# Mixing stage: two rotation tables scaled later, first swaps in PSUM, index pairs and value transposes later, top-k rounds spread

## Chip, cores and metric

One NeuronCore of one Trainium2 chip. The metric is the device time of one execution, in microseconds. TensorE is PE, VectorE is DVE, ScalarE is ACT and GpSimd is POOL in the rows.

## What is computed

Two blocks in a row on 512 tokens of width 1024. The first has a gated MLP, banded attention and two squared-ReLU MLPs. The second has two SwiGLU MLPs, a gated projection, and between the MLPs the mixing stage that this change is about. Cut to what matters:

```python
z = rms_norm_2(h, mix_norm) @ w_in
(aq, ak, av, iq, ik, iw, rq, rk, rv, rg, ga, gb) = jnp.split(z, split_points, axis=-1)
aq, ak, iq, ik = rope(aq), rope(ak), rope(iq) * 64 ** -0.5, rope(ik)      # 8, 1, 8, 1 heads of 64
rel = relu(einsum('bqhd,bsd->bqhs', iq, ik)); score = einsum('bqhs,bqh->bqs', rel, iw * 8 ** -0.5)
sel = top_k(where(admissible, score, -1e30), 128)                         # n_sel = min(256, 512 // 4)
y_a = softmax(aq @ ak[sel] / 8) @ av[sel]
rq, rk = rope(rq), rope(rk)                                               # 4 heads of 128
y_r = group_norm_heads(retention(rq, rk, rv)) * silu(rg)
merged = sigmoid(ga) * (y_a @ w_branch_a) + sigmoid(gb) * (y_r @ w_branch_b)
h = h + merged @ w_out
```

`rope` multiplies each head by a cosine and adds its swapped halves times a sine. The top 128 of up to 512 scores of a query are found in 16 rounds of 8.

## The kernel before

Activations lie feature-major: 128 features by 512 tokens a tile. Weights come as units of 128 x 1024 in fp32, are split into a high and a low part, and each product is three matmul passes (high x high, low x high, high x low; lines 435 to 437) over 8 tiles of contraction: 24 matmuls of 512 columns into one PSUM bank (`product`, `three_passes`). Most units are split by ScalarE (high) and VectorE (low). Units 256 to 294, those of the mixing stage up to the gates, are split by POOL: `high = raw * 1` (line 378) and `low = raw - high` (line 381), as soon as PE has finished the unit that held the slot before. SyncE's queue loads the raw units.

The engines run programs of their own that meet in semaphores; no scheduler stands between them, so the order of work on each engine is the order in the code. Four banks (0 to 3) take the units in turn: unit u waits until unit u - 4 is evacuated (semaphore `evacuated`).

On PE the mixing stage runs like this. First the units of the index queries (heads 0 to 3), of the index key (4) and of value and index weight (5, "avw"). Then units 6 to 10 (attention queries and key), with index work between their 40 tiles (`beside_heads`): one transposition of the value/weight unit (`transpose_avw`, line 760, bank 7) and 16 index pairs (`index_pair`, line 774, banks 4 to 7; four pairs for each of four query tiles t, with 128, 256, 384 and 512 keys). Then come eight retention units `ret_qk`, the retention values as two halves of four units each (`half_by_banks`, line 505, banks 0 to 3, bank by bank), and the gate stage: for each of four heads two gate units, retention scores, values (line 827) and transposes of the normalized result (line 838). The sparse attention stage follows.

VectorE evacuates each rotated unit in three instructions: `cosine_part` (line 1647, the unit's bank times the cosine table into T), then, after ScalarE's `swap_halves` (line 1170: copies of 32 or 64 rows from the unit's bank to `swapped(n)`), `sine_part`: the swapped half times the sine table (line 1652, frees the unit's bank) and the sum (line 1654). `swapped(n)` is a tile of T in SBUF for n below 10 and PSUM bank 4 or 5 for the retention units. The four tables `ROT` are first multiplied by the norm's reciprocal, which lies spread in PSUM bank 5 (line 1639). Line 1662 evacuates the value/weight unit. Index pairs pass through ScalarE's ReLU (line 1183, four buffers) and VectorE's `index_adds` (lines 1677, 1680), which sum 8 heads for each t into SC and then fill the inadmissible corner (line 1684). ScalarE copies SC to MK. `take(first, rounds)` is the top-k: a round is one maximum of 8 (line 1704) and one replacement (line 1705); rounds 0 to 15 work on 256 keys, 16 to 31 on 384, 32 to 47 on 512. `token_major(half, VT)` evacuates a value half in four instructions (line 1572). In the gate stage `mask(t)` turns SC and MK into an additive mask (lines 1723, 1725, 1726) ahead of `ret_norm(h)` (line 1761 writes YN).

Of the kernel before, what the change touches and what calls it, by code (L numbers as in the profile page):

```python
# [23 lines left out]
ALU = mybir.AluOpType  # L24
# [7 lines left out]
TT = SEQ // P  # L32
# [3 lines left out]
HD = 64  # L36
# [62 lines left out]
PAIRS = 4  # L99
# [58 lines left out]
def program(nc, xT, weights, gains, cols, lng, lnb, bs, wsT, rel, pos, ident_d, decay, pT, out):  # L158
    with ExitStack() as ctx:
        def at(name, kb, shape, dt=F32):  # L160
            return nc.alloc_sbuf_tensor_at(name, shape, dt, offset=16512 + int(kb * 1024))
# [15 lines left out]
        AQIQ = at("AQIQ", 64, [P, 8, SEQ])  # L177
        AK = at("AK", 80, [P, SEQ])
# [43 lines left out]
        ROT = at("ROT", 188, [P, 4, SEQ])  # L222
# [11 lines left out]
        COS64, SIN64, COS128, SIN128 = (ROT[:, n, :] for n in range(4))  # L234

        PS = ctx.enter_context(nc.psum_tensor("PS", [P, 8, SEQ], F32))

        def sem(name):
            return ctx.enter_context(nc.semaphore(name))
# [28 lines left out]
        dve_self, act_self = sem("dve_self"), sem("act_self")  # L268
# [32 lines left out]

        def swapped(n):

            return T[:, n % 2 * 2 + 1, :] if n < 10 else PS[:, 4 + n % 2, :]

        def ret_bank(c):
# [3 lines left out]
        def n_of(t):  # L310

            return P * (t + 1)
# [93 lines left out]
        def _(pe):  # L406
# [304 lines left out]
            for s in range(steps + 1):  # L711
                j = 2 * DT + 2 + 4 * s
# [50 lines left out]
            def index_pair(m):  # L763

                t, a = divmod(m, PAIRS)
                if m == 0:
                    pe.wait_ge(rotated, 5)
                if m == 1:
                    pe.wait_ge(index_ready, 1)
                if m >= 2:  # L770
                    pe.wait_ge(relu_done, 2 * m - 2)
                for hh in range(2):
                    r = slice(hh * HD, hh * HD + HD)
                    nc.tensor.matmul(PS[:, 4 + m % 2 * 2 + hh, 0:n_of(t)], AQIQ[r, 4 + a, t * P:t * P + P],
                                     IK[r, 0:n_of(t)], start=True, stop=True).then_inc(index_done, 1)

            def beside_heads(j):

                if j == 1:
                    transpose_avw()  # L780
                if j % 2 == 1 and j // 2 < TT * PAIRS:
                    index_pair(j // 2)
            for s in range(5):
                product(DT, XH, XL, after=lambda k: beside_heads(s * DT + k))
            for s in range(8):
# [112 lines left out]
            for s in range(first_step, last_step + 1):  # L898
                j = 4 * (s - first_step)
# [50 lines left out]
        def _(act):  # L950
# [3 lines left out]
            ta, me = Count(to_act), Count(act_self)  # L954
# [174 lines left out]
            for s in range(DT * TT):  # L1129
                p, t = divmod(s, TT)  # L1130
# [45 lines left out]
            def relus(first, last):  # L1176

                for n in range(first, last):
                    t = n // 8
                    act.wait_ge(index_done, n + 1)  # L1180
                    if n >= 4:
                        act.wait_ge(index_added, n - 3)
                    S.activation(RELU[:, n % 4, 0:n_of(t)], PS[:, 4 + n % 4, 0:n_of(t)], ACT.Relu)\
                     .then_inc(relu_done, 1)
            relus(0, 10)
            for t in range(TT):
                swap_halves(5 + t, heads + 6 + t, 32)
                act.wait_ge(scores_masked, t + 1)
                if t:
                    c = slice(off(t), off(t) + n_of(t))  # L1190
                    S.activation(MK[:, c], SC[:, c], ACT.Copy).then_inc(work_copied, 1)
                relus(8 * t + 10, min(8 * t + 18, 32))
            swap_halves(9, heads + 10, 32)
            for n in range(8):
                swap_halves(10 + n, FIRST["ret_qk"] + n, 64)
# [38 lines left out]
            for s in range(first_step, last_step):  # L1234
                p, t = divmod(s - first_step, TT)
# [63 lines left out]
        def _(dve):  # L1299
            dve.sem_inc(evacuated, SLOTS)  # L1300
            V = nc.vector
            done = Count(units_done, SLOTS)
            me, ao, ss = Count(dve_self), Count(act_out), Count(ss_ready)
# [294 lines left out]
            for s in range(DT * TT):  # L1598
                p, t = divmod(s, TT)
                n = n_of(t)  # L1600
# [34 lines left out]
            recip()  # L1635
            sp_.next()
            dve.wait_ge(ri_copied, rc.next())
            for n in range(4):
                V.tensor_tensor(ROT[:, n, :], ROT[:, n, :], PS[:, 5, :], ALU.mult).then_inc(dve_self, 1)
            dve.wait_ge(dve_self, me.next(4))  # L1640

            def cosine_part(n, cos, scale):


                if n >= 2:
                    dve.wait_ge(rotated, n - 1)
                V.scalar_tensor_tensor(T[:, n % 2 * 2, :], unit(), scale, cos, ALU.mult, ALU.mult).then_inc(turned, 1)

            def sine_part(n, dst, sin, scale):

                dve.wait_ge(act_out, ao.next())
                V.scalar_tensor_tensor(swapped(n), swapped(n), scale, sin, ALU.mult, ALU.mult).then_inc(evacuated, 1)
                dve.wait_ge(evacuated, FIRST["mix_heads"] + n + 1 + (n > 4) + SLOTS)
                V.tensor_tensor(dst, swapped(n), T[:, n % 2 * 2, :], ALU.add).then_inc(rotated, 1)

            cosine_part(0, COS64, HD ** -0.5)
            for n in range(4):
                cosine_part(n + 1, COS64, HD ** -0.5 if n < 3 else 1.0)
                sine_part(n, AQIQ[:, 4 + n, :], SIN64, HD ** -0.5)
            sine_part(4, IK[:], SIN64, 1.0)  # L1660
            dve.wait_ge(rotated, 4)
            V.tensor_tensor(T[:, 2, :], unit(), RI[:], ALU.mult).then_inc(evacuated, 1)
# [6 lines left out]
            def index_adds(t, first, last):  # L1669

                s = SC[:, off(t):off(t) + n_of(t)]
                for h in range(first, last):
                    n = 8 * t + h
                    w = AVW[:, t, HD + h:HD + h + 1]
                    dve.wait_ge(relu_done, n + 1)
                    if h == 0:
                        V.tensor_scalar(s, RELU[:, n % 4, 0:n_of(t)], w, None, ALU.mult).then_inc(index_added, 1)
                    else:
                        dve.wait_ge(index_added, n)
                        V.scalar_tensor_tensor(s, RELU[:, n % 4, 0:n_of(t)], w, s, ALU.mult, ALU.add)\  # L1680
                         .then_inc(index_added, 1)
                if last == 8:
                    dve.wait_ge(index_added, 8 * t + 8)
                    V.memset(s[0:CH, n_of(t) - CH:n_of(t)], NEG).then_inc(scores_masked, 1)
            index_adds(0, 0, 8)
            for t in range(TT):
                cosine_part(5 + t, COS64, HD ** -0.5)
                if t < TT - 1:
                    index_adds(t + 1, 0, 2)
                sine_part(5 + t, AQIQ[:, t, :], SIN64, HD ** -0.5)  # L1690
                if t < TT - 1:
                    index_adds(t + 1, 2, 8)
            cosine_part(9, COS64, 1.0)
            sine_part(9, AK[:], SIN64, 1.0)

            def take(first, rounds):


                for r in range(first, first + rounds):
                    t = 1 + r // 16  # L1700
                    if r % 16 == 0:
                        dve.wait_ge(work_copied, t)
                    work = MK[:, off(t):off(t) + n_of(t)]
                    link(V.max(TOP[:], work))  # L1704
                    link(V.match_replace(work, TOP[:], work, TAKEN))  # L1705

            for n in range(8):
                scale = 1.0 if n % 2 == 0 else P ** -0.5
                cosine_part(10 + n, COS128, scale)
                take(3 * n, 2)  # L1710
                sine_part(10 + n, R1[:, n, :], SIN128, scale)
                take(3 * n + 2, 1)
            take(24, 15)
            token_major(0, VT)
            take(39, 9)
            token_major(1, VT)

            def mask(t):


                c = slice(off(t), off(t) + n_of(t))
                ok = SC[:, c]
                link(V.tensor_scalar(ok, ok, 0.5 * NEG, None, ALU.is_gt))
                if t:
                    link(V.scalar_tensor_tensor(ok, MK[:, c], 0.5 * TAKEN, ok, ALU.is_lt, ALU.mult))
                V.tensor_scalar(MK[:, c], ok, -NEG, NEG, ALU.mult, ALU.add).then_inc(dve_self, 1)
                me.next()
# [12 lines left out]
            def two_bank_unit(u, dst):  # L1740

                dve.wait_ge(units_done, done.next())
                assert done.n == u + 1 + SLOTS
                V.tensor_tensor(dst, PS[:, 2 + u % 2, :], RI[:], ALU.mult).then_inc(evacuated, 1)
# [35 lines left out]
            ret_decay(0)  # L1780
            for h in range(4):
                two_bank_unit(rg0 + 2 * h, GT[:, 2 * h % 4, :])
                mask(h)
                ret_norm(h)
                two_bank_unit(rg0 + 2 * h + 1, GT[:, (2 * h + 1) % 4, :])
                if h < 3:
                    ret_decay(h + 1)
                ret_gated(h)
# [9 lines left out]
            for s in range(first_step, last_step):  # L1798
                p, t = divmod(s - first_step, TT)
                n = n_of(t)  # L1800
# [209 lines left out]
```

## Time and profile before

| | |
|---|---|
| runs | 2521.54 us median of 3 (2517.85 to 2522.76) |
| profiled execution | 2520.23 us, span 2518.4 us |
| mean granted clock of TensorE | 0.976 |
| busy share of the span | PE 95%, VectorE 54%, ScalarE 31%, POOL 18% |
| chain that ended last | PE 83%, VectorE 11%, ScalarE 3%, issue 2% |

The rotated units, values and gates of the mixing stage lie at about 1602 to 1854 us of the span. Times in the rows are from the span's start. The busy time of PE is modelled at the end of each matmul, so start-to-start distances say more than its busy share. A row of a timeline ends with the idle time of the engine before it and with what ended that.

### The profile page before, as it was taken

Reading aid. Unit: us, or ns where it says so; the run is one execution under the profiler, and the core shown is the slowest. Engines: PE = TensorE matmul, PEld = TensorE weight load, DVE = VectorE, ACT = ScalarE, POOL = GpSimd, SP = SyncE. Lnnn points to the kernel's source line nnn. Section 1 sums busy time; section 2 is a strip of 40 time slices with the busy share of each in tenths; the row PEclk is TensorE's granted clock in tenths of the full one; section 3 lists DMA queues with packets and bytes.
Section 4 is the critical chain, followed back from the end, with each engine's and each line's share of the span. In section 5 each row is a group of like instructions: output and inputs, shape, how many; then the busy total and the mean of one; then the engine's idle time right before and its main releaser. Section 6 shows DMA issues by size and latency. Waiting matters only on the chain.

```text
span 2518.4 us, 28995 instructions
## 1 busy us (share of the span) xinstructions
PE 2399.2 (95%) x10924; PEld 1934.3 (77%) x10924; DVE 1370.1 (54%) x1951; ACT 783.0 (31%) x1242; POOL 446.5 (18%) x203
## 2 busy tenths in 40 slices
PE   6789999997999899999999999998999999999997
PEld 5677888876766788888788888766877888888886
DVE  5666444446467644434555435789664454444465
ACT  2114323222233333223332223341244343222233
POOL 6670000003545200000000000456540000000000
PEclk8899999997999999999999999999999999999999
DMA  4232433321222233333143332223211343333221
GB/s 169 68 91 67 117 99 94 96 71 50 83 81 84 67 105 96 93 98 102 53 118 100 99 89 81 74 67 93 67 55 55 100 127 91 109 94 99 86 78 54
DMA packets 64833, 221.94 MB, mean 88 GB/s; under 512 B 7504, under 2 KB 9680, under 8 KB 64592
## 3 DMA queue, kind: packets, MB, share of 16 engines
q1 hardware_dynamic: 59184, 208.17, 27.9%
q10 hardware_dynamic: 5536, 12.19, 1.5%
q8 instruction: 80, 1.31, 0.2%
q14 instruction: 33, 0.27, 0.0%
HBM read 218.23 MB, written 2.10 MB: 87 GB/s over the span
## 4 chain that ended last, share of the span: by engine, by line
PE 83%; DVE 11%; ACT 3%; issue 2%; DMA 0%; POOL 0%; ACTq 0%; DVEq 0%; POOLq 0%
PE PS L435 23%; PE PS L437 22%; PE PS L436 22%; PE PS L454 3%; PE PS L531 2%; PE PS L458 1%; DVE SS L1344 1%; DVE MK L1705 1%; PE PS L681 1%; DVE SC L1680 1%; PE PS L505 1%; PE PS L702 1%; PE PS L691 1%; DVE TOP L1704 1%; PE PS L827 1%
## 5 line engine op out<-in xcount | busy, mean ns | idle before, releaser
L435 PE MATMUL PS<-XH,WH 128*128 128x512 f32 x1632 | 647.2, 397 | 19.6 <-DVE T L1542 12.5
L437 PE MATMUL PS<-XH,WL 128*128 128x512 f32 x1632 | 637.0, 390 | 0.0
L436 PE MATMUL PS<-XL,WH 128*128 128x512 f32 x1632 | 636.6, 390 | 0.0
L1332 DVE TENSOR_TENSOR WL<-RAW,WH 128x1024 fp32r<-128x1024 f32 (+3 forms) x308 | 362.2, 1176 | 224.3 <-ACT WH L977 219.7
L378 POOL TENSOR_TENSOR WH<-RAW,ONES 128x1024 fp32r<-128x1024 f32 x91 | 182.7, 2008 | 1437.3 <-DVE WL L1332 735.9
L977 ACT ACTIVATE WH<-RAW 128x1024 fp32r<-128x1024 f32 (+3 forms) x312 | 315.2, 1011 | 354.6 <-DVE M L1449 202.4
L435 PEld LDWEIGHTS PS<-XH,WH 128*128 128x128 f32 x1632 | 307.2, 188 | 101.3 <-issue 22.8
L435 PE MATMUL PS<-HH,WH 128*128 128x512 f32 x928 | 364.1, 392 | 2.6 <-DVE HL L1418 2.6
L437 PE MATMUL PS<-HH,WL 128*128 128x512 f32 x928 | 361.4, 389 | 0.0
L436 PE MATMUL PS<-HL,WH 128*128 128x512 f32 x928 | 361.2, 389 | 0.0
L437 PEld LDWEIGHTS PS<-XH,WL 128*128 128x128 f32 x1632 | 307.1, 188 | 65.1
L436 PEld LDWEIGHTS PS<-XL,WH 128*128 128x128 f32 x1632 | 307.5, 188 | 60.8
L381 POOL TENSOR_TENSOR WL<-RAW,WH 128x1024 fp32r<-128x1024 f32 x91 | 226.6, 2490 | 7.1
L435 PEld LDWEIGHTS PS<-HH,WH 128*128 128x128 f32 x928 | 174.2, 188 | 47.6 <-issue 9.1
L437 PEld LDWEIGHTS PS<-HH,WL 128*128 128x128 f32 x928 | 174.2, 188 | 36.5
L436 PEld LDWEIGHTS PS<-HL,WH 128*128 128x128 f32 x928 | 174.3, 188 | 35.2
L1418 DVE TENSOR_TENSOR HL<-T,HH 128x512 fp32r<-128x512 f32 x108 | 74.8, 692 | 127.4 <-ACT HH L1040 92.7
L1344 DVE TENSOR_TENSOR SS<-SS,T 128x512 f32<-128x512 f32 x91 | 85.0, 934 | 24.6 <-ACT T L983 24.6
L1037 ACT ACTIVATE T<-T 128x512 f32<-128x512 f32 x64 | 40.5, 632 | 185.0 <-DVE T L1425 185.0
L1449 DVE TENSOR_TENSOR M<-PS,M 128x512 f32<-128x512 f32 x48 | 33.1, 691 | 107.2 <-PE PS L437 106.8
L1052 ACT ACTIVATE HH<-T 128x512 fp32r<-128x512 f32 x44 | 27.8, 632 | 184.8 <-DVE T L1440 184.8
L1425 DVE SCALAR_TENSOR_TENSOR T<-PS,RI 128x512 f32<-128x512 f32 x64 | 44.2, 690 | 69.6 <-PE PS L437 61.6
(237 smaller groups left out, 2732.8 us busy)
## 6 DMA issues: line engine op xcount, KB each, us to landing
RAW<-in_weights SPq DMA_DIRECT2D x379, 512.0 KB, 3.5
RAW<-in_weights SPq DMA_DIRECT2D x16, 384.0 KB, 3.1
H<-in_xT ACTq DMA_DIRECT2D x8, 256.0 KB, 8.4
BIAS<-in_rel ACTq DMA_DIRECT2D x8, 256.0 KB, 3.5
RAW<-in_weights SPq DMA_DIRECT2D x8, 256.0 KB, 2.6
out<-R ACTq DMA_DIRECT2D x8, 256.0 KB, 2.2
BIAS<-in_rel ACTq DMA_DIRECT2D x8, 224.0 KB, 3.9
DECAY<-in_decay ACTq DMA_DIRECT2D x1, 1024.0 KB, 4.9
```

What stands on the lines that cost most here:

```text
L378: nc.gpsimd.tensor_tensor(high[:, 0:w], raw, ONES[:, 0:1].to_broadcast([P, w]), ALU.mult).then_inc(high_split, 1)
L381: nc.gpsimd.tensor_tensor(low[:, 0:w], raw, high[:, 0:w].bitcast(F32), ALU.subtract).then_inc(weights_split, 1)
L435: nc.tensor.matmul(PS[:, bank_, :], high[:, w], xh[:, k, :], start=(k == 0), stop=False)
L436: nc.tensor.matmul(PS[:, bank_, :], high[:, w], xl[:, k, :], start=False, stop=False)
L437: return nc.tensor.matmul(PS[:, bank_, :], low[:, w], xh[:, k, :], start=False, stop=stop)
L454: nc.tensor.matmul(PS[:, (first + s) % SLOTS, :], part[:, w], xh[:, k, :], start=(k == 0 and n == 0), stop=False)
L531: last = nc.tensor.matmul(PS[:, (first + j) % SLOTS, :], x[:, k, tok], wt[:, w], start=(k == 0 and x is XH and wt is high), stop=(k == DT ...
L977: S.activation(weights_of(u)[0][:, 0:w], RAW[:, slot, 0:w], ACT.Copy).then_inc(high_split, 1)
L1332: V.tensor_tensor(low[:, 0:w], RAW[:, slot, 0:w], high[:, 0:w].bitcast(F32), ALU.subtract).then_inc(weights_split, 1)
L1344: V.tensor_tensor(SS[:], SS[:], T[:, slot, :], ALU.add).then_inc(ss_ready, 1)
L1418: V.tensor_tensor(HL[:, f, :], T[:, src, :], HH[:, f, :].bitcast(F32), ALU.subtract).then_inc(h_ready, 1)
L1425: V.scalar_tensor_tensor(T[:, 0, :], src, 0.0, RI[:], ALU.max, ALU.mult)\
```

## The change

Six edits, all between 1602 and 1854 us. `swapped(n)` is PSUM bank 4 or 6 for n below 5 instead of a tile of T. The value transposes stand after tile 3 instead of tile 1 of unit 6, and index pair m after tile 2m + 3 instead of 2m + 1. ScalarE does 12 ReLUs instead of 10 ahead of its swap for unit 6. VectorE scales two of the four tables before the first unit and the other two after head 3. Of each row of eight index adds, four instead of two stand ahead of a unit's sine part. The 48 rounds of the top-k, before 24 among the retention units, 15 ahead of the first value half's evacuation and 9 behind it, are now 4 beside the last two of units 6 to 10, 16 among the retention units, 12 ahead of and 9 behind the first value half's evacuation, and 4 and 3 in the first two heads of the gate stage. The function `take` itself is the same.

```diff
@@ -301,6 +301,8 @@
 
         def swapped(n):
 
+            if n < 5:
+                return PS[:, 4 + n % 2 * 2, :]
             return T[:, n % 2 * 2 + 1, :] if n < 10 else PS[:, 4 + n % 2, :]
 
         def ret_bank(c):
@@ -776,10 +778,10 @@
 
             def beside_heads(j):
 
-                if j == 1:
+                if j == 3:
                     transpose_avw()
-                if j % 2 == 1 and j // 2 < TT * PAIRS:
-                    index_pair(j // 2)
+                if j % 2 == 1 and 0 <= j // 2 - 1 < TT * PAIRS:
+                    index_pair(j // 2 - 1)
             for s in range(5):
                 product(DT, XH, XL, after=lambda k: beside_heads(s * DT + k))
             for s in range(8):
@@ -1182,14 +1184,14 @@
                         act.wait_ge(index_added, n - 3)
                     S.activation(RELU[:, n % 4, 0:n_of(t)], PS[:, 4 + n % 4, 0:n_of(t)], ACT.Relu)\
                      .then_inc(relu_done, 1)
-            relus(0, 10)
+            relus(0, 12)
             for t in range(TT):
                 swap_halves(5 + t, heads + 6 + t, 32)
                 act.wait_ge(scores_masked, t + 1)
                 if t:
                     c = slice(off(t), off(t) + n_of(t))
                     S.activation(MK[:, c], SC[:, c], ACT.Copy).then_inc(work_copied, 1)
-                relus(8 * t + 10, min(8 * t + 18, 32))
+                relus(8 * t + 12, min(8 * t + 20, 32))
             swap_halves(9, heads + 10, 32)
             for n in range(8):
                 swap_halves(10 + n, FIRST["ret_qk"] + n, 64)
@@ -1635,9 +1637,9 @@
             recip()
             sp_.next()
             dve.wait_ge(ri_copied, rc.next())
-            for n in range(4):
+            for n in range(2):
                 V.tensor_tensor(ROT[:, n, :], ROT[:, n, :], PS[:, 5, :], ALU.mult).then_inc(dve_self, 1)
-            dve.wait_ge(dve_self, me.next(4))
+            dve.wait_ge(dve_self, me.next(2))
 
             def cosine_part(n, cos, scale):
 
@@ -1657,6 +1659,9 @@
             for n in range(4):
                 cosine_part(n + 1, COS64, HD ** -0.5 if n < 3 else 1.0)
                 sine_part(n, AQIQ[:, 4 + n, :], SIN64, HD ** -0.5)
+            for n in (2, 3):
+                V.tensor_tensor(ROT[:, n, :], ROT[:, n, :], PS[:, 5, :], ALU.mult).then_inc(dve_self, 1)
+            dve.wait_ge(dve_self, me.next(2))
             sine_part(4, IK[:], SIN64, 1.0)
             dve.wait_ge(rotated, 4)
             V.tensor_tensor(T[:, 2, :], unit(), RI[:], ALU.mult).then_inc(evacuated, 1)
@@ -1682,17 +1687,6 @@
                 if last == 8:
                     dve.wait_ge(index_added, 8 * t + 8)
                     V.memset(s[0:CH, n_of(t) - CH:n_of(t)], NEG).then_inc(scores_masked, 1)
-            index_adds(0, 0, 8)
-            for t in range(TT):
-                cosine_part(5 + t, COS64, HD ** -0.5)
-                if t < TT - 1:
-                    index_adds(t + 1, 0, 2)
-                sine_part(5 + t, AQIQ[:, t, :], SIN64, HD ** -0.5)
-                if t < TT - 1:
-                    index_adds(t + 1, 2, 8)
-            cosine_part(9, COS64, 1.0)
-            sine_part(9, AK[:], SIN64, 1.0)
-
             def take(first, rounds):
 
 
@@ -1704,15 +1698,28 @@
                     link(V.max(TOP[:], work))
                     link(V.match_replace(work, TOP[:], work, TAKEN))
 
+            index_adds(0, 0, 8)
+            for t in range(TT):
+                cosine_part(5 + t, COS64, HD ** -0.5)
+                if t < TT - 1:
+                    index_adds(t + 1, 0, 4)
+                else:
+                    take(0, 2)
+                sine_part(5 + t, AQIQ[:, t, :], SIN64, HD ** -0.5)
+                if t < TT - 1:
+                    index_adds(t + 1, 4, 8)
+            cosine_part(9, COS64, 1.0)
+            take(2, 2)
+            sine_part(9, AK[:], SIN64, 1.0)
+
             for n in range(8):
                 scale = 1.0 if n % 2 == 0 else P ** -0.5
                 cosine_part(10 + n, COS128, scale)
-                take(3 * n, 2)
+                take(4 + 2 * n, 2)
                 sine_part(10 + n, R1[:, n, :], SIN128, scale)
-                take(3 * n + 2, 1)
-            take(24, 15)
+            take(20, 12)
             token_major(0, VT)
-            take(39, 9)
+            take(32, 9)
             token_major(1, VT)
 
             def mask(t):
@@ -1780,6 +1787,8 @@
             ret_decay(0)
             for h in range(4):
                 two_bank_unit(rg0 + 2 * h, GT[:, 2 * h % 4, :])
+                if h < 2:
+                    take((41, 45)[h], (4, 3)[h])
                 mask(h)
                 ret_norm(h)
                 two_bank_unit(rg0 + 2 * h + 1, GT[:, (2 * h + 1) % 4, :])
```

## Rows read from the trace of the kernel before

**Rows 1.** Windows: busy us and count by engine, clock, DMA share, GB/s.

```profile
1602.00:1630.00 28.00, 24.09 (x116) 19.16 (x115) 19.40 (x24) 13.94 (x24) 9.07 (x4) 1.00 0.10 34
1630.00:1672.00 42.00, 37.06 (x158) 21.50 (x159) 32.17 (x41) 19.17 (x44) 18.18 (x9) 1.00 0.17 51
1672.00:1719.40 47.40, 47.40 (x211) 39.21 (x210) 40.51 (x80) 13.39 (x23) 36.38 (x17) 1.00 0.30 89
1719.40:1755.20 35.80, 25.68 (x97) 19.71 (x95) 34.15 (x77) 3.56 (x5) 19.86 (x10) 0.86 0.33 103
1755.20:1777.30 22.10, 22.05 (x97) 18.30 (x98) 14.83 (x30) 0.00 (x0) 14.47 (x7) 1.00 0.24 72
```

**Rows 2.** PE's waits, 1600 to 1780: total us, times, longest.

```profile
PE PS L505 <- DVE PS L1652: 7.3, 2, 3.9
PE PS L774 <- ACT RELU L1183: 4.9, 4, 1.6
PE PS L505 <- DVE VT L1572: 2.9, 1, 2.9
PE PS L760 <- DVE T L1662: 2.1, 1, 2.1
PE PS L435 <- DVE T L1652: 1.8, 1, 1.8
```

**Rows 3.** VectorE's timeline, heads: start, us, instruction, idle before.

```profile
1607.71 2.48 DVE L1639 TENSOR_TENSOR ROT<-ROT,PS 128x512 f32<-128x512 f32 x4 [3.31 <-ACT RI L1016]
...
1613.38 0.69 DVE L1652 SCALAR_TENSOR_TENSOR T<-T,ROT 128x512 f32<-128x512 f32 x1 [1.86 <-ACT T L1170]
...
1620.66 1.81 DVE L1652 SCALAR_TENSOR_TENSOR T<-T,ROT 128x512 f32<-128x512 f32 x1
1622.50 2.77 DVE L1654 TENSOR_TENSOR AQIQ<-T 128x512 f32<-128x512 f32 x1
...
1628.09 0.68 DVE L1662 TENSOR_TENSOR T<-PS,RI 128x512 f32<-128x512 f32 x1
...
1636.28 3.82 DVE L1680 SCALAR_TENSOR_TENSOR SC<-RELU,AVW,SC 128x128 f32<-128x128 f32 x2 [1.20 <-ACT RELU L1183]
```

**Rows 4.** POOL's timeline beside head 3's sine and sum.

```profile
1622.00 2.72 POOL L381 TENSOR_TENSOR WL<-RAW,WH 128x1024 fp32r<-128x1024 f32 x1
```

**Rows 5.** Tile PS on VectorE: ns shortest/median/longest, first and last start.

```profile
L1647 DVE SCALAR_TENSOR_TENSOR T<-PS,ROT x8: 684/692/692, 1692.5 to 1728.0; 128x512 f32<-128x512 f32 x8
L1652 DVE SCALAR_TENSOR_TENSOR PS<-PS,ROT x8: 699/699/700, 1695.1 to 1731.1; 128x512 f32<-128x512 f32 x8
...
L1572 DVE TENSOR_SCALAR VT<-PS,RT x1: 751/751/751, 1754.3 to 1754.3; 128x512 f32<-128x512 f32 x1
```

**Rows 6.** Tile TOP, the rounds of the top-k, same columns.

```profile
L1704 DVE MAX8 TOP<-MK x48: 416/561/696, 1693.1 to 1769.1; 128x8 f32<-128x256 f32 x16, 128x8 f32<-128x384 f32 x16, 128x8 f32<-128x512 f32 x16
...
L1705 DVE MATCH_REPLACE8 MK<-TOP,MK x48: 408/542/679, 1693.7 to 1769.9; 128x256 f32<-128x256 f32 x16, 128x384 f32<-128x384 f32 x16, 128x512 f32<-128x512 f32 x16
```

**Rows 7.** ScalarE's timeline: swaps of heads, of a retention unit.

```profile
1610.95 9.65 ACT L1170 ACTIVATE T<-PS 32x512 f32<-32x512 f32 x16 [3.35 <-DVE T L1647]
...
1693.25 1.15 ACT L1170 ACTIVATE PS<-PS 64x512 f32<-64x512 f32 x2 [3.45 <-DVE T L1647]
```

**Rows 8.** Tile SC: fills behind the adds, last mask instruction.

```profile
L1684 DVE MEMSET SC<- x4: 112/112/112, 1640.2 to 1679.1; 64x64 f32 x4
...
L1726 DVE TENSOR_SCALAR MK<-SC x4: 293/394/2397, 1787.0 to 1844.9; 128x128 f32<-128x128 f32 x1, 128x256 f32<-128x256 f32 x1, 128x384 f32<-128x384 f32 x1, 128x512 f32<-128x512 f32 x1
```

**Rows 9.** PE's timeline in the first value half.

```profile
1732.48 0.63 PE L505 MATMUL PS<-WL,XH 128*128 128x512 f32 x1
```

**Rows 10.** Timelines of the gate stage, head 0: POOL, VectorE, PE.

```profile
1786.97 2.35 POOL L381 TENSOR_TENSOR WL<-RAW,WH 128x1024 fp32r<-128x1024 f32 x1
...
1791.59 1.90 DVE L1761 TENSOR_SCALAR YN<-PS,MV,RSD 128x256 f32<-128x256 f32 x4
...
1796.71 1.04 PE L838 MATMUL PS<-IDENT,YN 128*128 128x128 f32 x8
```

## Prediction

> **What bounds the kernel now.** I read the page's chain first, for who sets the end; then the granted clock and the busy times by stretch, to find where TensorE (PE) is not full; then PE's waits in the mixing stage; then the VectorE, POOL and ScalarE timelines around each of these waits. The chain is mostly PE, and VectorE for most of the rest; the reader is to see in [rows 1] where the rest lies. Of five stretches of the mixing stage PE is full in two and not full in three: the end of the statistics and the first heads (1602 to 1630), the index pairs (1630 to 1672), and the first value half (1719.4 to 1755.2), which also ran at a mean granted clock of 0.86. Elsewhere in this stage a shorter VectorE instruction buys nothing.
>
> The waits of PE in it are nine [rows 2]: 1.8 us for the first head's evacuation, 2.1 for the value/weight unit's evacuation ahead of its transposes, 4.9 in four pieces for index pairs that find the ReLU late, 7.3 in two for the evacuations of the last two retention units, 2.9 once for the first value half's evacuation. All are released by VectorE, or by ScalarE behind VectorE. So the question for every edit is whether VectorE gets to one of these places sooner, and what else it gets to later.
>
> VectorE is late for two reasons. One is its list of work. The other stands in [rows 3, 4]: a sine product with both inputs in SBUF takes 0.69 us at 1613.38, but 1.81 at 1620.66, and the sum after it 2.77 at 1622.50, ending 0.55 us after POOL's low split (1622.00 + 2.72). Two index adds beside a later pair of POOL's take 3.82 where they need 0.8. The retention units' instructions, one input in PSUM, show 0.68 to 0.70 in all 16 cases of cosine and sine while POOL works beside them [rows 5]; the rounds hold to their lengths too (the three values of a row are its three widths, not a scatter) [rows 6].
>
> **The change, part by part.**
>
> *Two tables later.* The four multiplications take 2.48 us, the next instruction starts 2.5 us after the first [rows 3]; two of them out of the way start head 0's cosine 1.2 us sooner, and the swap, the sine and PE's wait follow. So the wait of 1.8 becomes 0.6: **-1.2**. The other two run after head 3's sum, 1.2 us of VectorE there; what that delays is the next paragraph's.
>
> *First swaps in PSUM.* The swap's place changes, so that head 0 to 4's sine and sum read one input from PSUM. That frees two rows outright: 1.81 + 2.77 become 1.4 (3.2 us), and head 4's sum, held in the same way ahead of 1628.09, loses 1.6. ScalarE's price: 16 copies of 32 rows took 9.65 us, 0.60 each, and two of 64 rows from PSUM to PSUM 1.15, 0.58 each [rows 7]; below 0.1 us a swap, taken as nothing. The Trainium skill (ScalarE: Activation LUTs, Step-by-step: what each stage is for) calls ScalarE's way to PSUM the faster one; by these rows it is faster by 0.02 us a copy, which would add 0.1 to the sum.
>
> *The value/weight unit.* New times in this part are on the clock of the old trace. Head 4's matmuls start 1.2 sooner and end at 1618.8; VectorE evacuates (cosine) to 1619.4, sine and sum of head 3 to 1620.8, the two tables to 1622.05, head 4's sine and sum (swap done 1622) to 1623.5. Its evacuation then waits for PE's unit, done at 1624.2, and ends at 1624.9 instead of 1628.8 (1628.09 + 0.68). PE asks for it four tiles after 1624.1, which at 0.68 us a tile (three matmuls of 47.40/211 = 0.225, [rows 1]) is 1626.8. No wait: **-2.1**. The two tiles done earlier are not lost, they are missing later.
>
> *Index pairs and ReLUs.* PE issues pair m two tiles later in its own order, 1.4 us, and its own time is 3.3 us earlier, so pairs come about 2.0 us before the old ones. VectorE's adds follow. POOL starts a pair of splits (1.9 + 2.7) at each unit's end, now at 1631.6, 1640, 1649.3, 1659.5, 1667.3. Laying VectorE's list beside them, each instruction with two SBUF inputs waiting for the split that runs: adds of block 0 end at 1637.2 (old 1640.2), block 1 at 1647.1, block 2 at 1656.9, block 3 at 1668 to 1670 (old 1679.1; these two from the fills that follow the adds, [rows 8]). The splits mostly hit the sine and the sum of a head instead of a row of adds, because four adds now stand ahead of it. The ReLU which a pair needs is there 2 to 4 us before the pair (pair 9 at 1646.8, its ReLU at 1643.4; pair 12 at 1654.1, 1652.2; pair 15 at 1662.1, 1658.6). ScalarE's 12 ReLUs ahead of the first swap instead of 10 delay that swap by 1 us, inside this. So all four waits go: **-4.9**. The lower bound is none of them (a split that lands on the adds again), the upper is all.
>
> *Rounds.* A round costs 0.98, 1.25 or 1.52 us at 256, 384 or 512 keys (maximum + load + replace less overlap [rows 6]). Before: 24 rounds sit among the retention units, 15 ahead of the first value evacuation, 9 after it. Now 4 sit beside heads 8 and 9, 16 in the retention units, 12 ahead of the first evacuation, 9 behind it, 7 in the gates. So 7 rounds of 512 (10.6 us) and some 10 us of stalls leave VectorE's list ahead of the first value half. VectorE reaches the first retention unit at 1678.4 (old 1692.5, [rows 5]) and needs 3.9 us a unit (0.6 + 2 x 0.98 + 1.4) where PE makes one in 5.45; from the fifth on it waits for PE. The last unit: cosine, two rounds of 1.25, sine end 4.0 us after PE finished it; PE needs that bank 18 matmuls into the value half, 4.1 us. Both waits (3.9 and 3.3) go. The 12 rounds of 384 then take 15.0, to 19.8 us into a half of 21.8; VectorE is idle when the half ends, and PE waits only for the first evacuation, 0.75 us [rows 5] and the hand-over: 0.9 instead of 2.9. With no wait and the clock whole, this stretch has the length of the second half: 35.8 against 22.1 us for the same 97 matmuls [rows 1]. So 13.7 - 0.9 = **-12.8**, of which 3.4 is the clock: some 15 matmuls here start 0.43 us apart, not 0.23, and show 0.63 us as the one at 1732.48 does [rows 9]. That is the 1.2 GHz level, after PE had stood 3.9 us. The waits of 1.8 and 2.1 lie in a stretch with granted clock 1.00, and the one of 2.9 is followed by one with 1.00 [rows 1], so 0.9 should not bring it.
>
> *Rounds in the gates.* 4 x 1.52 = 6.1 us before the first mask, 3 x 1.52 = 4.6 before the second. VectorE's normalization of head 0 ends at 1793.24, PE asks for it at 1796.71 to 1796.88: 3.6 us of room; 2.7 in head 1 (1812.33 against 1815.02, the same pattern 18.3 us on) [rows 10]. By that alone PE would wait 2.5 and 1.9 us. But the masks give time back. Of the four last mask instructions the median is 0.39 us [rows 8] and the longest, head 0's, 2.40: it began at 1787.01 beside a low split that began at 1786.97 and ended at 1789.3 [rows 10]. The compare ahead of it (1.4) ended with the high split. The new rounds outlast both splits, so head 0's mask costs 0.6 instead of 3.8, head 1's 1.1 instead of 4.3; net 2.9 and 1.4 more, within 3.6 and 2.7. **0**; bounded by +4.4 if the masks keep their old length. The rule for this is in the Trainium skill (SBUF — State Buffer, SBUF: two separate sides): VectorE in a two-port mode and GpSimd take a shared port pair by an exclusive lock, held for a whole instruction. By it the mask is short once POOL is idle and the sum stands; by the mean of the rows as they are, it would be 4.4 us less gain. The nine rounds behind the first evacuation keep their 6 us of idle before the second one ends.
>
> **Sum.** -1.2 - 2.1 - 4.9 - 12.8 = -21.0 us. The profiled execution took 2520.23 us (span 2518.4): 2499.2. The median of the runs is 1.3 us above it, 2500.5. Everything behind the gates is PE-bound or hangs on PE's counts, so it only moves.
>
> **Rivals.**
> 1. *The splits still hit the adds.* POOL's starts are tied to unit ends, VectorE's adds to pairs; an error of 2 us in my laying puts a 4.6 us stall on a row of adds. Against: 2 to 4 us of room. Then two to four index waits stay, up to 4.9, and nothing later, since VectorE has 7 us or more of room before the fifth retention unit: 2503 to 2505.5.
> 2. *The gates become the bound.* If the masks stay at 3.8 and 4.3, PE waits 2.5 + 1.9: 2505.
> 3. *The list is still too long.* If VectorE got to the retention units 12 us later than I have it, it would keep the last evacuations behind PE by some us and the low clock with them: a gain of 8 to 12, 2509 to 2513.
> 4. *Slower.* The gates, now without idle on VectorE in heads 0 and 1, wait as in rival 2 and lose the 2.4 GHz level there. A matmul then costs 0.43 instead of 0.23 us. To eat the gain of 21 and 5 more, past the 4.4 us of waiting, it takes 110 matmuls (five of the eight gate units) at the low level. The only stay at it in this stage held 15 matmuls. It decides only if the level stays down through most of the gates.
> 5. *Only the seven rounds' move does anything:* the PSUM swaps are neutral, since the ends of heads 0 to 2 are not beside POOL. Then 2.1 is halved and part of the index waits stay: 2503, inside rival 1.
>
> **How the numbers follow.** Forecast 0.74; rivals 1 and 5 together 0.13; 2, 0.07; 3, 0.04; 4, 0.02. The likeliest alone runs from 2498 (the swap's and hand-overs' few tenths more) to 2502. The range reaches down to 2497 (the three runs span 5 us, so a median of a few can sit 1 off) and up through rivals 1, 2 and 5 to 2507. 0.2% is 5 us, about what a measurement can tell from no change; all cases but rival 4 gain more: faster 0.97, same 0.01, slower 0.02.
>
> **What would show it.** Head 4 of the mixing stage starts some 1.2 us sooner with a wait near 0.6; the transposes of the value/weight unit and the index pairs without a wait; sine and sum of heads 0 to 4 all near 0.7; retention units' cosines spaced 5.45 from the fifth on; granted clock 1.00 through the value halves; one PE wait near 0.9 between them; head 0's mask under 1 us and no wait before the gate stage's transposes. Wrong would be: waits for a ReLU in the index stage, a wait for YN in the gates, or a clock under 1.00 anywhere between 1700 and 1800.

## The result and the profile after

| | median | runs |
|---|---|---|
| before | 2517.85 us | 2512.71 to 2522.76 (5) |
| changed | 2498.86 us | 2493.56 to 2499.06 (5) |

The ratio is 0.9916 with a 95% interval from 0.9897 to 0.9935: 16 to 26 us of 2518. The median lies inside the stated range, 1.6 us below the forecast. The profiled execution of the changed kernel took 2493.56 us (span 2491.8), 26.7 less than the profiled one of before, and only two thirds of that belong to the change.

To keep the parts apart I use three lengths of every trace. The *start* is VectorE's first table multiplication. The *stage* goes from there to PE's first retention score; the *gates* from there to the first sparse score; the *rest* to the end.

| profile | start | stage | gates | rest |
|---|---|---|---|---|
| before | 1607.7 | 169.4 | 73.3 | 668.0 |
| before, again | 1598.9 | 169.3 | 73.3 | 667.9 |
| changed | 1598.3 | 151.4 | 73.3 | 668.7 |
| changed, again | 1599.3 | 151.5 | 73.3 | 668.8 |

So the change gave 17.9 us in the stage (18.0 and 17.8 in the two pairs). The forecast's sum was 21.0. The 9.4 us that the first pair of profiles shows ahead of the stage is scatter: a second profile of the kernel before starts it at 1598.9, and the mean granted clock ahead of the stage was 0.969 in the first and 0.977 in the second.

The rest is 0.8 longer in both profiles of the changed kernel. PE's waits in it add up to the same 6.5 us in all four, but the 1.2 GHz level in which every profile of the kernel ends begins 12.2 and 12.3 us before the end of the span there, and 9.8 and 9.7 us in the two of before. Of all the profiles of this study, three have a rest of 668.0 or less and that level for the last 9.7 to 9.9 us: the two of before and the one with the rounds as before. The ten others have 668.6 to 669.3 and 12.0 to 13.9 us. So the loss goes with the rounds' new places; why they bring the level sooner stays open.

The windows of the changed kernel, with the columns of [rows 1] (the stage starts 9.4 us earlier here): the heads, the index pairs, the end of the retention units with the first value half, the second half.

```profile
1592.60:1620.60 28.00, 27.47 (x133) 21.88 (x131) 16.25 (x27) 14.08 (x27) 8.56 (x4) 1.00 0.12 38
1620.60:1662.60 42.00, 42.00 (x180) 26.19 (x179) 36.53 (x41) 20.10 (x44) 22.55 (x10) 1.00 0.20 62
...
1700.00:1728.00 28.00, 24.88 (x110) 19.99 (x109) 24.30 (x58) 3.56 (x5) 19.95 (x10) 1.00 0.41 119
1728.00:1750.00 22.00, 22.00 (x97) 18.20 (x98) 14.68 (x30) 0.00 (x0) 16.16 (x8) 1.00 0.29 88
```

The index pairs' window is full where PE had 37.06 of 42 us, and no window shows a clock under 1.00. PE's waits, the answer to [rows 2]:

```profile
PE PS L507 <- DVE PS L1654: 2.1, 1, 2.1
PE PS L507 <- DVE VT L1574: 1.0, 1, 1.0
PE PS L437 <- DVE T L1654: 0.8, 2, 0.5
PE PS L437 <- DVE PS L1654: 0.5, 1, 0.5
```

The nine waits have become five, 19 us have become 4.4. The last line is the first head (forecast 0.6), the second the value half's evacuation (0.9). The first and the third, 2.9 us, were not forecast. VectorE's timeline shows where they come from (lines 1654 and 1656 are sine and sum, 1685 the adds, 1649 the cosine):

```profile
1610.00 0.69 DVE L1654 SCALAR_TENSOR_TENSOR PS<-PS,ROT 128x512 f32<-128x512 f32 x1
1610.72 0.69 DVE L1656 TENSOR_TENSOR AQIQ<-PS,T 128x512 f32<-128x512 f32 x1
...
1614.83 0.69 DVE L1667 TENSOR_TENSOR T<-PS,RI 128x512 f32<-128x512 f32 x1 [0.77 <-PE PS L439]
...
1637.94 0.11 DVE L1689 MEMSET SC<- 64x64 f32 x1
...
1639.83 4.89 DVE L1685 SCALAR_TENSOR_TENSOR SC<-RELU,AVW,SC 128x384 f32<-128x384 f32 x2
...
1650.06 5.94 DVE L1685 SCALAR_TENSOR_TENSOR SC<-RELU,AVW,SC 128x512 f32<-128x512 f32 x3
...
1657.24 6.78 DVE L1685 SCALAR_TENSOR_TENSOR SC<-RELU,AVW,SC 128x512 f32<-128x512 f32 x4
1664.09 0.11 DVE L1689 MEMSET SC<- 64x64 f32 x1
...
1677.29 0.68 DVE L1649 SCALAR_TENSOR_TENSOR T<-PS,ROT 128x512 f32<-128x512 f32 x1
```

The two rows at 1610 are those of [rows 3] that took 1.81 and 2.77. Up to the fill at 1637.94 (forecast 1647.1 - 9.4 = 1637.7) VectorE is where I laid it. Then the adds are hit, that is, they start while a split of POOL's runs and last until it ends: two take 4.89 where they need 1.3, three 5.94 where they need 2.4, four 6.78 where they need 3.3. POOL's splits at those times:

```profile
1649.91 1.89 POOL L380 TENSOR_TENSOR WH<-RAW,ONES 128x1024 fp32r<-128x1024 f32 x1 [5.61 <-PE PS L439]
1651.88 2.71 POOL L383 TENSOR_TENSOR WL<-RAW,WH 128x1024 fp32r<-128x1024 f32 x1
1657.92 1.89 POOL L380 TENSOR_TENSOR WH<-RAW,ONES 128x1024 fp32r<-128x1024 f32 x1 [3.33 <-PE PS L439]
1659.90 2.72 POOL L383 TENSOR_TENSOR WL<-RAW,WH 128x1024 fp32r<-128x1024 f32 x1
```

The splits stand within 0.3 us of the forecast (1659.5 - 9.4 and 1667.3 - 9.4); it is the instruction beside them that I had wrong. By the last fill (1664.09) VectorE is 3.5 to 5.5 us behind the forecast (1668 to 1670, less 9.4). The rest of the delay comes at heads 8 and 9, whose sines and sums are hit too, four instructions that need 2.8 us:

```profile
1667.37 1.44 DVE L1654 SCALAR_TENSOR_TENSOR T<-T,ROT 128x512 f32<-128x512 f32 x1 [0.70 <-ACT T L1172]
1668.84 2.40 DVE L1656 TENSOR_TENSOR AQIQ<-T 128x512 f32<-128x512 f32 x1
...
1674.37 0.69 DVE L1654 SCALAR_TENSOR_TENSOR T<-T,ROT 128x512 f32<-128x512 f32 x1 [0.69 <-ACT T L1172]
1675.10 2.27 DVE L1656 TENSOR_TENSOR AK<-T 128x512 f32<-128x512 f32 x1
```

VectorE reaches the first retention unit's cosine 78.9 us after the stage's start, where the forecast has 70.7 and before 84.8.

In the gate stage, head 0 (the answer to [rows 8, 10]), VectorE's timeline and then PE's; line 1733 is the last mask instruction, 1768 writes YN, 840 transposes it:

```profile
1764.25 0.23 DVE L1730 TENSOR_SCALAR SC<-SC 128x128 f32<-128x128 f32 x1
1764.51 0.23 DVE L1733 TENSOR_SCALAR MK<-SC 128x128 f32<-128x128 f32 x1
...
1766.93 1.90 DVE L1768 TENSOR_SCALAR YN<-PS,MV,RSD 128x256 f32<-128x256 f32 x4
```

```profile
1767.19 2.32 PE L817 MATMUL PS<-R 128*128 128x512 f32 x8
1769.35 1.04 PE L840 MATMUL PS<-IDENT,YN 128*128 128x128 f32 x8
```

The mask took 0.5 us instead of 3.8, YN ends at 1768.83, PE asks for it at 1769.35: no wait, with 0.5 us left.

### The profile page after: what moved, and what is told of

Read it like the earlier page. It is cut to its first block, busy times and chain, and to the rows that moved or that the text cites. A ratio compares the mean times of both kernels' runs of the same rounds, so it can differ in the third digit from the quotient of the medians.

```text
span 2491.8 us, 28996 instructions
## 1 busy us (share of the span) xinstructions
PE 2388.7 (96%) x10924; PEld 1926.5 (77%) x10924; DVE 1353.8 (54%) x1951; ACT 782.9 (31%) x1242; POOL 446.4 (18%) x203
## 4 chain that ended last, share of the span: by engine, by line
PE 86%; DVE 9%; ACT 3%; issue 2%; POOL 0%; DMA 0%; ACTq 0%; DVEq 0%; POOLq 0%
PE PS L437 23%; PE PS L439 23%; PE PS L438 22%; PE PS L456 3%; PE PS L533 3%; PE PS L507 2%; PE PS L460 1%; PE PS L683 1%; DVE SC L1685 1%; DVE SS L1346 1%; PE PS L704 1%; PE PS L693 1%; PE PS L829 1%; DVE WL L1334 1%; ACT WH L979 1%
## 5 line engine op out<-in xcount | busy, mean ns | idle before, releaser
L1054 ACT ACTIVATE HH<-T 128x512 fp32r<-128x512 f32 x44 | 27.8, 632 | 184.8 <-DVE T L1442 184.8
```

## Experiments

All stand beside the changed kernel's 151.4 us of stage, 73.3 of gates and 78.9 to the first retention cosine ("arrival"). "Waits" is what PE waits in the stage, 4.4 in the changed kernel. Each row is one profile.

| kernel | waits | arrival | stage | gates |
|---|---|---|---|---|
| rounds alone | 10.4 | 84.9 | 157.4 | 73.3 |
| rounds as before | 12.6 | 78.9 | 163.4 | 73.3 |
| swaps in SBUF | 7.7 | 83.9 | 158.0 | 73.3 |
| pairs early | 7.9 | 82.5 | 155.0 | 73.3 |
| tables as before | 5.6 | 80.1 | 154.2 | 73.3 |
| adds by two | 4.5 | 78.6 | 151.1 | 73.3 |
| mask first | 4.4 | 78.9 | 151.5 | 79.2 |
| ReLU in PSUM | 5.2 | 74.5 | 151.7 | 73.3 |
| last swaps in PSUM | 1.5 | 74.7 | 147.8 | 73.3 |

**Which edit carries what.** Six kernels undo one edit each, or make one alone. Their code is shortened; two of them stand further down.

```diff
 # swaps in SBUF (changed kernel, but)
-            if n < 5:
-                return PS[:, 4 + n % 2 * 2, :]
 # pairs early
-                if j == 3:
+                if j == 1:
                     transpose_avw()
-                if j % 2 == 1 and 0 <= j // 2 - 1 < TT * PAIRS:
-                    index_pair(j // 2 - 1)
+                if j % 2 == 1 and j // 2 < TT * PAIRS:
+                    index_pair(j // 2)
 # rounds as before: take(3 * n, 2), take(3 * n + 2, 1), take(24, 15), take(39, 9), none elsewhere
 # rounds alone: the kernel before with take(0, 2), take(2, 2), take(4 + 2 * n, 2), take(20, 12),
 #               take(32, 9) and take((41, 45)[h], (4, 3)[h]) at the places of the changed kernel
```

> The changed kernel with the swaps of heads 0 to 4 back in SBUF. Stage length here and below: from VectorE's first table multiplication to PE's first retention score, 169.6 us before, 151.6 in the changed kernel. Theory (a VectorE instruction with two SBUF inputs stands still for the POOL split that runs): sine and sum of heads 3 and 4 take 1.8 to 2.8 us again, the value/weight unit is evacuated some 3.5 us later, PE waits about 2 us ahead of its transposes, the adds start 2 us later, the last waits grow with them: stage 153.5 to 157.5. Rival (the swaps' place is neutral): 151.6.

Measured 158.0, 0.5 above the range. The held instructions are back, and PE waits 3.2 us for the value/weight unit. The waits grew by only 3.3 and the stage by 6.6; the other 3 are the clock. Head 3's sum in VectorE's timeline, and then two windows, one behind that wait and one later:

```profile
1612.54 2.77 DVE L1654 TENSOR_TENSOR AQIQ<-T 128x512 f32<-128x512 f32 x1
```

```profile
1622.00:1627.00 5.00, 5.00 (x20) 3.47 (x20) 2.21 (x6) 0.89 (x4) 0.00 (x0) 0.66 0.21 82
...
1712.00:1720.00 8.00, 5.84 (x19) 4.31 (x18) 7.62 (x19) 1.86 (x3) 3.30 (x3) 0.79 0.58 197
```

Mean granted clock 0.66 and 0.79: part of these 5 and 8 us ran at 1.2 GHz. The rival (place neutral) falls.

> The changed kernel with transposes and index pairs back after tiles 1 and 2m + 1. Theory (VectorE's earlier arrival alone brings the ReLUs in time, room 2 to 4 us against 1.4 us of shift): at most one or two waits under 1 us in the index stage, stage 151.6 to 153. Rival (the shift is what removed the four waits): they return, 155 to 156.5.

Measured 155.0. No pair waited for a ReLU, so the shift is not what removed the four waits, and the rival falls. The theory was right on the waits of the index stage (one of 0.7 us, for the index weights) and 2 us short on the stage: the splits come at other places of VectorE's list, its arrival is 3.6 us later, and PE waits 3.6 us for the evacuations of the last heads, where the changed kernel waits 0.8. These 2.8 and the 0.7 are what the stage is longer by.

> The changed kernel with the 48 rounds where they were before (24, 15, 9). Theory (VectorE's list ahead of the first value half sets the waits there): last retention unit evacuated some 6 us late, first value half's evacuation some 4.5 us late, granted clock possibly low in between: stage 158 to 163. Rival (the earlier edits alone already give VectorE enough room): 151.6 or less, since four rounds fewer stand ahead of the retention units.

Measured 163.4, 0.4 above the range; the theory is right in kind. PE waits 8.5 us for the last three retention units and 3.0 for the value half. So the other edits without the rounds give 6.0 us. The clock between the waits, two windows:

```profile
1717.00:1721.00 4.00, 1.26 (x3) 0.45 (x2) 3.79 (x11) 1.14 (x2) 0.00 (x0) 0.50 0.00 0
1721.00:1725.00 4.00, 3.42 (x8) 2.77 (x9) 3.83 (x9) 1.28 (x1) 0.41 (x1) 0.50 0.43 119
```

> The kernel before with only the rounds moved (4, 16, 12, 9, 4, 3). Theory: the waits ahead of the index stage and in it stay (1.8, 2.1, 4.9); the last retention unit's evacuation is 4.6 us late instead of 7.3 in all, the value half's 0.9; the low clock may stay for a part: stage 161.5 to 164.5 of 169.6. Rival (rounds are worth all of it): 153.

Measured 157.4, 4 us under the range: 12.0 us of 17.9 come with the rounds alone, more than I expected, and with the 6.0 above they make the whole. All early waits stayed (1.8, 2.1, 5.0), but the last retention unit was only 0.6 us late, not 4.6, and no matmul of the stage ran at 1.2 GHz. My figure charged 3.9 us for the four rounds beside heads 8 and 9. The arrival is 84.8 without and 84.9 with them: they fill time in which VectorE waits for ScalarE's swap.

```diff
 # tables as before
-            for n in range(2):
+            for n in range(4):
                 V.tensor_tensor(ROT[:, n, :], ROT[:, n, :], PS[:, 5, :], ALU.mult).then_inc(dve_self, 1)
 # and no second loop over (2, 3) behind head 3
 # adds by two: index_adds(t + 1, 0, 2), index_adds(t + 1, 2, 8), relus(0, 10), relus(8 * t + 10, ...)
```

> The changed kernel with all four tables scaled ahead of the first cosine. Theory: the first wait of PE is 1.7 instead of 0.5 us, VectorE has its 0.8 us of idle ahead of the value/weight unit as cover, and everything behind moves by 1.2: stage 152.7. Rival (the later waits take it up): 151.5.

Measured 154.2, 2.8 more than the changed kernel and 1.5 more than expected. The first wait is 1.7 as expected; 1.2 is that wait. Most of the rest is clock: a wait of 2.1 us for the last retention unit, as long as in the changed kernel, is followed here by matmuls at the low level, there by none. The window around that wait:

```profile
1718.00:1724.00 6.00, 3.89 (x12) 2.84 (x11) 5.73 (x13) 1.70 (x2) 1.78 (x2) 0.75 0.59 175
```

The changed kernel's six microseconds around its wait (1706.5 to 1712.5) have 18 matmuls, at 1.00, where these have 12.

> The changed kernel with two adds and 10 ReLUs ahead of a sine part as before, PSUM swaps, later pairs and rounds kept. Theory (which instruction a POOL split holds decides VectorE's arrival): sine and sum stand at other places against the splits; arrival at the first retention unit changes by 2 us or more from 79.0 after the stage's start, and the last waits with it: stage 149.5 to 156. Rival (order of adds neutral): arrival and stage stay within 0.5 of 79.0 and 151.5.

Measured: arrival 78.6, stage 151.1. This rival holds for the sum, though not for its parts: two pairs wait for a ReLU again (2.4 us) and the waits at the end shrink by as much. Four adds ahead of the sine instead of two gain nothing (the stage is 0.3 us shorter with two), and the theory that the order would move the arrival by 2 us fell.

**Why instructions are long beside POOL.**

```diff
 # mask first
-                if h < 2:
-                    take((41, 45)[h], (4, 3)[h])
                 mask(h)
+                if h < 2:
+                    take((41, 45)[h], (4, 3)[h])
 # ReLU in PSUM
-                    S.activation(RELU[:, n % 4, 0:n_of(t)], PS[:, 4 + n % 4, 0:n_of(t)], ACT.Relu)\
+                    S.activation(PS[:, 4 + n % 4, 0:n_of(t)], PS[:, 4 + n % 4, 0:n_of(t)], ACT.Relu)\
# the adds read PS instead of RELU; pair m waits for adds (index_added, 2 * m - 2) instead of
# ReLUs, and a ReLU no longer waits for the add that frees its buffer
```

> The changed kernel with the gate stage's rounds behind mask 0 and mask 1 instead of ahead of them. Gate length, from PE's first retention score to its first sparse score: about 76 us before and now. Theory (masks are long only beside a POOL split): mask 0 takes 3.8 us and mask 1 4.3 again, PE waits 2.5 and 1.9 us ahead of the transposes of heads 0 and 1, gate length 4.4 more. Rival (masks got short for another reason): they stay at 0.5 and 1.0, no wait.

Measured: gates 79.2, 5.8 more. Head 0's last mask instruction takes 2.40 us as in [rows 8], and the one ahead of it 1.42, where in the changed kernel, behind the rounds, each takes 0.23. VectorE's timeline with the mask first:

```profile
1762.31 1.42 DVE L1730 TENSOR_SCALAR SC<-SC 128x128 f32<-128x128 f32 x1
1763.76 2.40 DVE L1733 TENSOR_SCALAR MK<-SC 128x128 f32<-128x128 f32 x1
```

PE's transposes of head 0 start 1.4 us late and take 1.5 longer, those of head 1 0.4 and 1.1: 4.4 us, the size that the theory gave. Most of the other 1.4 is the clock. In PE's timeline, behind the transposes of head 0, its matmuls start 0.43 us apart for a while:

```profile
1775.02 2.69 PE L840 MATMUL PS<-IDENT,YN 128*128 128x128 f32 x8 [1.38 <-DVE YN L1768]
1777.35 0.78 PE L437 MATMUL PS<-XH,WH 128*128 128x512 f32 x1
1777.93 0.63 PE L438 MATMUL PS<-XL,WH 128*128 128x512 f32 x1
```

That is rival 2 of the prediction, with a piece of rival 4 behind it: with the rounds behind the masks both would have come true.

> The changed kernel with the ReLU in place in PSUM, so that the index adds read one input from PSUM; a pair then waits for the adds of the pair two before it, not for its ReLU. Theory: no add is longer than 0.8 us whatever POOL does, VectorE reaches the retention units some 5 to 8 us sooner and the waits of 0.5 and 2.1 go; a pair behind a head's sine and sum may wait 1 to 2 us for adds, two or three times: stage 149 to 153. Rival (adds are long for another reason, ReLU or semaphores): the stalls of 2 to 5 us in the rows of adds stay.

Measured: stage 151.7. No add is longer than 0.8 us, whatever POOL does; the arrival is 4.5 us sooner, where 5 to 8 were expected, since the splits now hit the sums of heads 6 and 7 as well (2.8 and 2.7 us, where the changed kernel has 0.7); the last waits but that of the value half are gone; and two pairs wait 1.9 and 1.8 us for adds, as the theory has it. VectorE's timeline at the last four adds of block 0, which took 4.73 in the changed kernel:

```profile
1629.33 0.81 DVE L1683 SCALAR_TENSOR_TENSOR SC<-PS,AVW,SC 128x128 f32<-128x128 f32 x2 [1.20 <-ACT PS L1183]
1631.34 0.81 DVE L1683 SCALAR_TENSOR_TENSOR SC<-PS,AVW,SC 128x128 f32<-128x128 f32 x2 [1.21 <-ACT PS L1183]
```

**A faster version.**

```diff
-            return T[:, n % 2 * 2 + 1, :] if n < 10 else PS[:, 4 + n % 2, :]
+            return T[:, n % 2 * 2 + 1, :] if n < 8 else PS[:, 4 + n % 2, :]
```

> The changed kernel with the swaps of the last two of heads 5 to 9 in PSUM banks 4 and 5 as well (their index pairs are over by then). Theory (two-SBUF-input instructions held by POOL are why VectorE is 8 us later than I laid it out): sine and sum of these two fall from 6.8 to 2.8 us, VectorE reaches the first retention unit some 4 us sooner, PE's waits of 0.5 and 2.1 go: stage 149.0 against 151.6, gate stage unchanged. Rival (VectorE's list as such is too long, the instructions' place is neutral): 151.6.

Measured in five runs: 2495.26 us against 2516.22 before, ratio 0.9901 (0.9884 to 0.9918). The stage is 147.8, 3.6 less than the changed kernel's and 1.2 better than expected. The intervals of the two ratios overlap, so the whole times do not tell the two kernels apart; the stage's length, which repeats to 0.1 us, does. The rest is 0.5 longer (669.2), so 3.1 us of the 3.6 are left. The arrival is 4.3 us sooner and the two waits are gone; what is left is the first head's 0.5 and the value half's 1.0. A late head in VectorE's timeline, its swap now in PSUM:

```profile
1672.45 0.70 DVE L1654 SCALAR_TENSOR_TENSOR PS<-PS,ROT 128x512 f32<-128x512 f32 x1 [0.59 <-ACT PS L1172]
1673.19 0.69 DVE L1656 TENSOR_TENSOR AQIQ<-PS,T 128x512 f32<-128x512 f32 x1
```

**What is not the stage.**

> The changed kernel once more, to see what in the first profile is the stage's and what is other. Theory: stage length 151.6 again within 0.5; the start of the stage lies anywhere from 1598 to 1608 us, by the granted clock of the stages before it. Rival: the change itself moved the start by 9 us, then it lies at 1598 again.

> The kernel before once more, profiled. Theory: its stage length is 169.4 again within 0.5, and the point at which the stage starts scatters over some 8 us with the granted clock of the stages ahead of it, as it does among the changed kernels (1598 to 1605 us); it may lie well below the 1607.7 of the first profile. Rival (the change moved the start): it lies above 1605 again.

The stage lengths came out as both theories have them (the table at the top). The changed kernel's second start, 1599.3, did not tell its theory from its rival, which names 1598 too; the second profile of before did, since it starts at 1598.9 without the change. Stage lengths repeat to 0.1 us, the start does not: it lay anywhere from 1598.3 to 1608.6 in the thirteen profiles of this study. A whole-time difference of two single executions can therefore be 9 us off; the stage's length is the finer measure.

## Why the prediction held, and where it did not

- *Tables, first wait (-1.2).* 1.8 became 0.5: 1.3.
- *Value/weight unit (-2.1).* Right; VectorE stood idle for 0.8 us ahead of its evacuation. Undoing the swaps brought a wait of 3.2 back.
- *Index pairs (-4.9).* All four waits went. The forecast gave the pairs' shift a part in it; with the pairs back in their old places no ReLU was late. What the shift changes is VectorE's place against the splits (3.6 us of arrival).
- *End of the list (-12.8).* This term was mis-sized: it measured 9.6 (17.9 less the 8.3 above). The step that failed is the laying of VectorE's list against the splits: "the splits mostly hit the sine and the sum of a head instead of a row of adds". In block 1 they did; in blocks 2 and 3 adds were hit, and at heads 8 and 9, where the forecast's times leave no room for a hit, sines and sums took 6.8 us instead of 2.8. VectorE arrived 8.2 us later than laid out, about half of it by the last fill and half at these two heads. PE kept a wait of 2.1 us for the last retention unit and 0.8 in two pieces. The ground given, "because four adds now stand ahead of it", did not hold either: with two adds the arrival was 0.3 us sooner.
- *The room.* Rival 1 says that VectorE has "7 us or more of room before the fifth retention unit". An estimate from two traces: with the last swaps in PSUM the last unit's cosine waits for PE and starts at 103.1 us of the stage; in the changed kernel it comes 27.8 us after the arrival (106.7 less 78.9). From the forecast's arrival of 70.7 that leaves 4.6 us, and the delay was 8.2. The same list without the hits on heads 8 and 9 has neither wait. So a part of rival 3 happened, at 3 us instead of 9 to 13.
- *Clock (3.4 us within the last term).* Right for this kernel: no matmul of the stage's products ran at 1.2 GHz. But the ground, that waits of about 2 us do not bring the low level, was wrong: two experiments fell to it after 2.2 and 2.1. As the changed kernel kept a wait of 2.1 that the forecast did not have, its full clock there is partly luck.
- *Gates (0).* Right, and by the mechanism given. The Trainium skill's rule of the exclusive port pair (SBUF — State Buffer, Who interferes with whom) agrees with the rows here: two inputs in SBUF (2.77) or an SBUF-to-SBUF `TENSOR_SCALAR` (2.40) held, one input in PSUM never (0.70), the same mask 0.23 once POOL is idle.
- *Sum.* 21.0 forecast, 17.9 in the stage. The medians differ by 19.0, and the median of the changed kernel came out 1.6 us under the forecast because the runs of before that it was built on were high by some 4 us: their median fell from 2521.54 (3 runs) to 2517.85 (5). That the median came so close is luck: a gain 3 us too large and a base 4 us too high nearly cancel.

## What to carry to other kernels

Where a POOL instruction of 2 to 3 us shares the time with VectorE, the place of an operand can weigh more than an instruction's own length: moving one input of four VectorE instructions (two heads' sines and sums) to PSUM took them from 6.8 us to 2.8 and cost ScalarE nothing. Fill work belongs where VectorE waits for another engine (four rounds there were free). Work that POOL does not hold belongs beside its splits, and work that it does hold behind them (5.8 us between the two orders of the same seven rounds and the masks). And when a stage is to be judged whose effect is under one per cent, its own length in two traces says more than the whole time.

## What the runs showed of the hardware

- What decides whether an instruction of VectorE's is held is which of the two starts first. Between the stage's start and the end of the gates, the thirteen profiles have 645 mask instructions and adds, sines and sums that read no PSUM. Of 236 that start while a split runs, 235 are held. Of 47 that start ahead of a split which begins beside them, one is (it starts 6 ns ahead). Of 362 without a split beside them, none is. No run takes the splits away, so that POOL is the cause rests on this timing and on the experiments that moved an operand or the order.
- The granted clock falls after shorter waits than the 3.9 us of before, and not each time: after 3.2 us and after 2.2 in the same run (windows at 0.66 and 0.79), after 1.4 and some tenths for the later transposes in the kernel with the mask first, but not after 2.1 in the changed kernel, nor after 2.7 with the pairs early. In the swaps' experiment it cost 3 us on top of 3.3 of waiting. So the length of the wait alone does not decide it; where in time the wait falls was not tried by itself.
- The rounds' `MAX8` and `MATCH_REPLACE8` on SBUF (0.41 to 0.70 us) were not held by POOL in any trace, `TENSOR_SCALAR` on SBUF was.
- ScalarE's swaps of 32 rows took 9.24 us for 16 into PSUM against 9.65 into SBUF. The Trainium skill (ScalarE: Activation LUTs, Step-by-step: what each stage is for) has this direction; it is 4% here.
